# Second expert's w1 product as one plain float32 product, and its split work on ScalarE and VectorE dropped

## The reference, cut to what matters

```python
def moe_ffn(h, router_w, router_b, w1, w3, w2):
    scores = sigmoid(h @ router_w)
    ...                                   # best group of 4 experts, best 2 of it, gates
    for e in range(16):
        he = silu(h @ w1[e]) * (h @ w3[e])        # w1, w3: 1024 x 512
        y = y + gates[:, e:e + 1] * (he @ w2[e])  # w2: 512 x 1024
    return y
```

## Time and profile before

| | before |
|---|---|
| median of 3 runs | 586.81 us (586.78 to 587.27) |
| the profiled execution | 587.05 us, its span 585.2 us |
| PE busy | 549.8 us, 94% of the span |
| DVE busy | 450.1 us, 77% |
| ACT busy | 325.1 us, 56% |
| POOL busy | 155.4 us, 27% |
| mean DMA rate | 294 GB/s |
| mean granted clock of PE | 0.985 |

### The profile page before, as it was taken

One profiled execution on the slowest core, in us unless ns is written; L12 is line 12 of the kernel. 1 busy time (PEld: TensorE's weight loads), 2 busy tenths in 40 slices (PEclk: granted clock), 3 DMA queues, 4 the chain that ended last, 5 costly groups with the idle time before them and its releaser, 6 DMA issues.

```text
span 585.2 us, 7667 instructions
## 1 busy us (share of the span) xinstructions
PE 549.8 (94%) x2733; PEld 417.7 (71%) x2733; DVE 450.1 (77%) x592; ACT 325.1 (56%) x405; POOL 155.4 (27%) x141
## 2 busy tenths in 40 slices
PE   1789999999998999989999899999999999999995
PEld 1345875677676787857687788888888888877772
DVE  1348699446586546477999899999999999989867
ACT  4541133535435922266586496677886676966624
POOL 5000833223310700020781321233311333200070
PEclk9799999999999999999999899999999999999998
DMA  8999994878224720149979999999999999999665
GB/s 295 390 372 318 378 379 178 275 207 316 73 72 157 239 73 37 60 160 390 342 282 392 393 324 393 393 392 393 392 387 391 390 393 390 361 375 361 201 217 214
DMA packets 88746, 171.81 MB, mean 294 GB/s; under 512 B 5379, under 2 KB 18887, under 8 KB 88721
## 3 DMA queue, kind: packets, MB, share of 16 engines
q1 hardware_dynamic: 82578, 153.34, 73.4%
q10 hardware_dynamic: 2768, 9.97, 4.2%
q0 software_dynamic: 3376, 8.18, 3.9%
HBM read 158.06 MB, written 17.32 MB: 300 GB/s over the span
## 4 chain that ended last, share of the span: by engine, by line
PE 80%; DMA 6%; DVE 6%; ACT 3%; issue 3%; SPq 1%; DVEq 0%; ACTq 0%
PE psum L896 6%; PE psum L1244 4%; PE psum L1246 4%; PE psum L1245 4%; PE psum L1271 4%; PE psum L1273 4%; PE psum L1272 4%; PE psum L1256 4%; PE psum L1255 4%; PE psum L1254 4%; PE psum L904 4%; DMA w<-in_moe_w 3%; PE psum L941 3%; DMA ada<-in_ada_w 3%; PE psum L943 3%; PE psum L942 3%
## 5 line engine op out<-in xcount | busy, mean ns | idle before, releaser
L2245 DVE TENSOR_TENSOR w_lo<-w,w_hi 128x2048 fp32r<-128x2048 f32 x32 | 72.9, 2282 | 1.2 <-ACT w_hi L1669 1.2
L2234 DVE TENSOR_TENSOR w_lo<-w,w_hi 128x1024 fp32r<-128x1024 f32 (+2 forms) x30 | 68.6, 2292 | 0.0
L1660 ACT CAST w_hi<-w 128x2048 fp32r<-128x2048 f32 x30 | 57.3, 1911 | 16.3 <-PE psum L1256 13.7
L1669 ACT CAST w_hi<-w 128x2048 fp32r<-128x2048 f32 x32 | 60.4, 1918 | 7.3 <-DVE ysb L2267 6.1
L2228 DVE TENSOR_TENSOR w_lo<-w,w_hi_a 128x2048 fp32r<-128x2048 f32 (+1 forms) x30 | 51.6, 1757 | 3.9 <-ACT w_hi_a L1648 3.4
L1271 PE MATMUL psum<-w_hi,heT_hi 128*128 128x512 f32 x120 | 49.8, 415 | 0.8 <-DVE w_lo L2245 0.8
L1851 DVE SCALAR_TENSOR_TENSOR rows<-ada,cc,rows 128x512 f32<-128x512 f32 x48 | 41.8, 874 | 8.9 <-DMA ada<-in_ada_w 7.4
L762 POOL COPY idx<-idx 128x1 int32 x12 | 9.9, 826 | 141.5 <-PE psum L1217 141.5
L1273 PE MATMUL psum<-w_hi,heT_lo 128*128 128x512 f32 x120 | 47.2, 394 | 0.0
L1272 PE MATMUL psum<-w_lo,heT_hi 128*128 128x512 f32 x120 | 47.1, 393 | 0.0
L1245 PE MATMUL psum<-w_lo,xgT_hi 128*128 128x512 f32 x120 | 46.8, 390 | 0.0
(11 more groups left out here) (368 smaller groups left out, 1271.6 us busy)
## 6 DMA issues: line engine op xcount, KB each, us to landing
w<-in_moe_w SPq DMA_DIRECT2D x32, 2048.0 KB, 13.5
w<-in_moe_w SPq DMA_DIRECT2D x32, 1024.0 KB, 13.8
ada<-in_ada_w SPq DMA_DIRECT2D x12, 2048.0 KB, 18.2
win<-in_w_in SPq DMA_DIRECT2D x8, 1024.0 KB, 14.5
expert_rows<-ysb ACTq DMA_DIRECT2D x15, 512.0 KB, 6.3
expert_rows<-zero SPq DMA_DIRECT2D x1, 5120.0 KB, 21.1
wout<-in_w_out SPq DMA_DIRECT2D x4, 1024.0 KB, 4.9
x<-in_x SPq DMA_DIRECT2D x2, 1024.0 KB, 10.0
```

The lines of the kernel that those rows point to most:

```text
L1669: act.copy(w2_hi[:, :, hs], w2_sb[b][:, :, hs]).then_inc(w2_hi_ok[half], 1)
L2234: v.tensor_tensor(w3_lo[b][:, ks, :], w3_sb[b][:, ks, :], w3_hi[:, ks, :], ALU.subtract).then_inc(w3_lo_ok, n)
L2245: v.tensor_tensor(w2_lo[b][:, :, hs], w2_sb[b][:, :, hs], w2_hi[:, :, hs], ALU.subtract).then_inc(w2_lo_ok[half], 1)
```

## The change

- PE: block 1's w1 product becomes `plain1_second`, eight plain float32 matmuls of `xgT_1` (the turned rows, unsplit) with `w1_sb[1]` as loaded. The turning of block 0's hidden rows stays in its middle. The wait for the low parts of block 1's rows moves behind the first w2 half product.
- ACT: the four casts of block 1's w1 go. A copy of the turned rows of block 1 from PSUM to `xgT_1` comes in ahead of their cast. The second cast of block 1's w3 moves ahead of the cast of block 0's hidden rows, and the four casts of block 2's w1 move ahead of the silu of block 1.
- DVE: the three instructions that make the low parts of block 1's w1 go. The low parts of both halves of block 0's w2 come directly behind `overflow_blocks`, ahead of the low part of block 1's rows. The first low part of block 1's w3 comes ahead of the low part of block 0's hidden rows. The first low part of block 2's w1 comes ahead of the first result rows.
- POOL and SP have the same lists as before. The semaphores that the dropped work raised are raised by hand.

```diff
+        xgT_1 = at("xgT_1", 180 * K1, [P, KD, P])
...
+            def plain1_second():
+                pe.wait_ge(w1_in[1], 16)
+                pe.wait_ge(x0_ok, KD + 1)
+                pe.wait_ge(sg_ok, 1)
+                for k in range(KD):
+                    if k == 4:
+                        hidden_turned(0)
+                    m = pe.matmul(bank[2][:], xgT_1[:, k, :], w1_sb[1][:, k, :], start=(k == 0), stop=(k == KD - 1))
+                m.then_inc(h1_ok, 1)
...
             overflow_index()
-            hidden1(1, 1, 0)
+            plain1_second()
             expert_out0(0, 0)
+            pe.wait_ge(x_lo_ok, 2)
             hidden3(1, 1)
...
-                if k == 6:
-                    act.wait_ge(w1_in[1], 16)
-                    high_w1_part(1, 0)
-                    high_w1_part(1, 1)
...
-            high_w1_part(1, 2)
-            high_w1_part(1, 3)
+            act.sem_inc(w1_hi_ok, 4)
             high_w2(0, 0, 0, 0)
             high_w2(0, 0, 0, 1)
             gate_half(0)
+            act.wait_ge(xt_ok, 2)
+            act.copy(xgT_1[:].rearrange("p k t -> p (k t)"), psum[:, 0:2, :].rearrange("p a n -> p (a n)")
+                     ).then_inc(x0_ok, 1)
             high_rows(1)
             act.wait_ge(w3_in[1], 16)
             high_w3(1, 0)
+            high_w3(1, 1)
             high_hidden(0, 0)
-            high_w3(1, 1)
+            act.wait_ge(w1_in[0], 32)
+            for g in range(4):
+                high_w1_part(0, g)
             gate_half(1)
-            high_w1(0, 2, 1)
             high_w2(1, 1, 0, 0)
...
-            low_w1(1, 1, 0, 2)
+            v.sem_inc(w1_lo_ok, 4)
             overflow_blocks()
-            low_w1(1, 1, 2)
-            low_w1(1, 1, 3)
+            low_w2(0, 0, 0)
+            low_w2(0, 0, 1)
             low_rows(1)
-            low_w2(0, 0, 0)
             gated(0)
             index(NE, NB, 2)
             v.tensor_copy(gslot[:], bank[6][:, 2 * OVER:2 * OVER + NB]).then_inc(idx_ok, 1)
             overflow_list()
+            low_w3(1, 1, 0, 2)
             low_hidden(0, 0)
-            low_w3(1, 1, 0, 2)
             low_w3(1, 1, 2, 2)
-            low_w2(0, 0, 1)
+            low_w1(0, 2, 0, 2)
             v.wait_ge(rows_act, 8)
             expert_rows(0, 0, 0, 0)
-            low_w1(0, 2, 0, 2)
             gated(1)
             low_w2(1, 1, 0)
             low_hidden(1, 1)
```

## The result

The changed kernel took 594.52 us (median of 4 runs, 592.55 to 597.82) against 587.04 us for the kernel before (4 runs, 586.78 to 587.76): a ratio of 1.0135, interval 1.0099 to 1.017. That is 7.5 us slower. The forecast was 4.7 us slower, with a range that ended at 592.9. Its sign and its account of the first part of the path were right; the size was too small. The profiled execution took 594.56 us with a span of 592.5, 7.3 us over the span before.

What follows compares the result with a forecast made beforehand. PE bounds the kernel until 302.2 us, then ACT's casts lead to DVE until 323.85. Product 1.3, POOL wait 1.7 and clock 1.7 make 4.7 us on 586.8, so 591.5 us; range 589.2 to 592.9.

Steps and rivals of the forecast that it cites:

- What follows on the path: Behind block 1's product: later loads, readers and DVE's 307.43 to 323.85 us stretch just move with PE; nothing added.
- the 2.5 us wait at 321.2 and its clock loss: PE's wait for DVE at the transposes of line 1264, forecast to stay unchanged and move with the rest.
- The product: Block 1's w1 product on PE with four transposes: 7.35 us plain against 6.05 split, 1.30 us more on the path.
- POOL's hold-up: DVE's two w2 subtractions stall POOL's hot_mod slices, so PE waits about 1.7 us at overflow_index.
- the 6.43 us row: POOL operation ending at 299.62 us beside unbroken DVE subtractions, its like taking 0.31; evidence that POOL cannot get between them.
- the 2.38 us slice: POOL's eighth hot_mod slice, 283.20 to 285.58 us, others 0.59; it ended 0.38 us after DVE's two subtractions.
- The clock behind the new wait: PE's clock falls after its wait for POOL and the 16 small matmuls, costing 1.7 us in plain1_second.
- The longer wait: Rival: DVE's low part of the rows also holds POOL; PE waits 2.9 us, clock falls, 592.7 us; chance 0.08.
- The clock's holding: Rival: PE's clock does not fall over its wait for POOL; 589.8 us; chance 0.25.

Runs made afterwards that it cites:

- three increments: Changed kernel with three semaphore increments that nobody waits for added to ACT's list ahead of the first rows: 588.73 us, ratio 1.0047.
- one increment: Changed kernel with a single empty semaphore increment more in ACT's list: 593.72 us, ratio 1.0103.
- two: Changed kernel with 2 empty semaphore increments more in ACT's list: 589.21 us, ratio 1.0047.
- filled: Changed kernel with one unused plain float32 matmul of 512 columns on PE ahead of overflow_index, where PE waited for POOL: 591.84 us, ratio 1.0105.
- the changed kernel again: Changed kernel as it is, with nothing altered, measured and profiled a second time: 594.1 us, ratio 1.0142.
- The relief: Changed kernel with three empty ACT increments, DVE held until POOL is done, and DVE's stretch ahead of PE's late wait shortened: 586.31 us, ratio 1.0008.
- shifted: Kernel before with four plain float32 matmuls of idle work on PE, 3.44 us, between overflow_index and block 1's w1 product: 589.61 us, ratio 1.0065.
- both undone: Changed kernel with three empty ACT increments and block 0's w2 low parts back behind the low part of block 1's rows: 586.89 us, ratio 1.0019.
- the kernel before, -3: Kernel before with two ACT increments given to POOL and two block 1 w1 casts made as one: 590.05 us, ratio 1.0074.
- DVE's order as before: Changed kernel with DVE's list in the kernel before's order, less the dropped block 1 w1 low parts: 592.28 us, ratio 1.0107.

## Why the prediction fell short, step by step

**Failed: "What follows on the path".** It said that the DVE stretch has the same instructions and is released the same way, "so the 2.5 us wait at 321.2 and its clock loss stay". DVE's instructions were the same; its input was not. The step looked at DVE's list and at what releases its first instruction, and not at ACT's list beside it, from which three instructions had gone. That put the store's turn (314.92) ahead of a packet of ACT's code (318.3), which in the kernel before had come 2.9 us ahead of the store; it is read from the runs with one, two and three increments. Against 0 forecast it cost 3.35 us of longer wait and 1.1 of clock by the profile. By the times it is 4.3 us (0.0074) where it is put on the kernel before by itself, 5.6 us of 8.3 (1.0142 - 1.0047) where three increments take it off, and 3.3 between one increment and two. I know of no row of the kernel before that would have given the number: its issue of 402 ns against a median of 343 is all that sets the store apart there. What could have been had is the warning that this path passes ACT, and that ACT was ahead of DVE there by only 1.7 us.

**The product: right.** 7.35 us forecast, 7.39 measured at full clock; alone it makes the kernel 1.1 us slower (ratio 1.0019, interval 1.0 to 1.0039) against 1.3.

**POOL's hold-up: right in kind, too large.** Undoing it gave 1.8 us in the first batch, and 1.6 between the kernels with three increments (1.0047 - 1.0019), where 1.7 + 1.7 = 3.4 were forecast. `overflow_blocks` took 6.3 us instead of 6.8 to 7.5, so the subtractions ran from 278.25 to 282.93 instead of 279.5 to 284.1, and POOL had no slice through ahead of them. But POOL came in between the two, where the prediction says that it does not (POOL's first two slices, then the cast of w2 that the second subtraction reads, and that subtraction):

```profile
278.33 2.68 POOL L772 TENSOR_SCALAR hot_mod<-iota_slot,stat 128x128 f32<-128x128 bf16 x1
```

```profile
281.01 2.39 POOL L772 TENSOR_SCALAR hot_mod<-iota_slot,stat 128x128 f32<-128x128 bf16 x1
```

```profile
278.71 1.90 ACT L1681 CAST w_hi<-w 128x2048 fp32r<-128x2048 f32 x1 [1.07 <-DMA w<-in_moe_w]
```

```profile
280.64 2.29 DVE L2257 TENSOR_TENSOR w_lo<-w,w_hi 128x2048 fp32r<-128x2048 f32 x1
```

The first slice ends some 0.5 us behind the first subtraction, not behind the second; the other six ran at 0.59. Had it been held for both, as I took from the 6.43 us row, the last slice would have ended 0.6 later. PE also followed at once (0.05 us) where I allowed 0.2 to 0.4, for which I had no row: at PE's waits in the kernel before it is 0.05 to 0.15. Together: 286.92 instead of 287.9, and a wait of 0.8 instead of 1.7.

The record points to the cast of w2 as what let POOL in. I had the casts of w2 start earlier and be done; in fact the second waited for its load and ended at 280.61, when DVE was through with the first subtraction, so that the second came 0.11 us behind its end (back to back, the record of the next starts 0.08 us ahead of the last one's end). Of the six profiles with these slices, the cast held the second subtraction up in four (first profile, filled, three increments, two), by 0.03 us or more, and POOL's first slice took 2.4 to 2.7 us. In the other two (the changed kernel again, one increment) nothing held it up, and that slice took 4.51 and 4.52 us: it was held for both. So it is with the 6.43 us row, which crossed two borders without a pause, and the 2.38 us slice, which crossed one.

That the pause decides is a reading of these eight rows, and no run set it on purpose. One profile speaks against it: in the kernel before with three instructions fewer, two subtractions stand back to back (the first ends at 282.29, the record of the second starts at 282.20), and the slice that had started at 280.87, 0.2 us ahead of the first of them, ended at 282.66, between the ends of the two.

**The clock behind the new wait: right in most profiles.** The 1.7 us of the forecast are the fall behind the 2.5 us wait in the kernel before, 3.4 us at 0.50 from 325.3 us on the earlier trace rows; the changed kernel shows the same amount, 3.4 us at 0.50 from 289.0 us on. It fell in four of the five profiles that have the wait (0.7 to 0.9 us there) and not in the fifth (1.2 us). A chance near 0.75 for the fall, rather than a certain term, was fair.

**The rivals.** None came true as written. The longer wait (592.7) had DVE's low part of the rows stop POOL: that was not put to the test, since that part runs from 286.40, when POOL is nearly done (286.87). The clock's holding (589.8) is near to what the three increments give (1.0047 of 586.8 is 589.6 us), but by another way: there the wait is 0.7 us and the clock falls. In one profile of the changed kernel the clock did hold over the new wait.

**Not foreseen: what the end gives back.** Of the 8.35 us of lateness at 353.56, 1.3 were gone by 550, about what the longer clock stretch had cost, since a block that had waited for transfers (in the kernel before the chain goes by a weight load until 516.80 us, and PE waits 0.9 us for `he` at 523.01) waited no more and took 17.9 us instead of 18.8. The relief shows the same from the other side.

## What to carry to other kernels

A change to one engine's list can move its later instructions against the packets that bring its code, as three instructions fewer did here on ACT (an issue of 5.06 us for one of 0.40). Where an exposed chain passes a DMA issue of that engine while the DMA engines are full (share 1.05 here), compare the longest issue of that line with its median in both kernels (402 and 5059 ns against 343 here), and pad the list by a few empty instructions before believing what the edit itself cost. When a step says that a stretch stays as it is, go through the lists of all engines that feed it, not only the one that the chain names. Before counting a gain in the middle as a gain at the end, check whether the transfers behind it set the pace (a lead of 2.2 us was 0.3 at 523 us here).

## What the runs showed of the hardware

- The issue of a store on ACT took 0.40, 1.22, or 4.97 to 5.15 us, with 322, 321, or 320 and 319 instructions executed ahead of it; three instructions that do nothing were worth 5.6 us of 594 (ratios 1.0142 and 1.0047, from two batches). In all seven profiles with an issue of over 1 us it ended 1.70 to 1.72 us behind the start of a packet of code on q14.
- TensorE's granted clock did not answer alike to like waits: behind a wait of 2.5 to 2.6 us for `he` it fell in two profiles (before, shifted) and held in three (three increments, two, both undone); behind the wait for `hot_mod` it fell after 0.7 to 0.9 us and held after 1.2.
- Beside two subtractions of DVE with both inputs in SBUF, 128x2048 each and back to back, one POOL slice of 0.59 us took 4.51 or 4.52 us; where the second subtraction came 0.03 to 0.3 us late, the slice ended after the first one, in 2.4 to 2.7 us. In one profile (the kernel before, -3) a slice ended between two that stood back to back, in 1.79 us. The eight slices took 4.68 us without the subtractions (DVE's order as before) and 8.2 to 8.6 with them.
